# Stick-breaking scores: two rounded products on 128 rows in place of one FP32 product on 64 rows

## The reference

```python
def stick_breaking_attention(q, k, v):          # 8 heads, 512 tokens, 64 wide, for each of 2 layers
    ...
    def block(args):
        qb, qpos = args
        mask = kpos[None, :] < qpos[:, None]
        z = jnp.einsum('bhqd,bhkd->bhqk', qb, k).astype(jnp.float32) * scale     # the scores
        log_beta = jax.nn.log_sigmoid(z)
        log_rem = jnp.where(mask, jax.nn.log_sigmoid(-z), 0.0)
        after = lax.cumsum(log_rem, axis=key_axis, reverse=True) - log_rem
        a = jnp.where(mask, jnp.exp(log_beta + after), 0.0)
        return jnp.einsum('bhqk,bhkd->bhqd', a.astype(v.dtype), v)
```

## Time and profile before

| what | value |
|---|---|
| median of 3 timed runs | 2813.29 us (2812.91 to 2813.4) |
| profiled execution, its span from first to last instruction | 2810.2 us |
| PE busy | 2791.2 us, 99% of the span |
| POOL busy | 2045.0 us, 73% |
| DVE busy | 1325.6 us, 47% |
| ACT busy | 816.3 us, 29% |
| granted PE clock | 0.999 of full speed |
| DMA | 242.59 MB, mean 86 GB/s |

### The profile page before, as it was taken

How to read it: one execution, slowest core, us unless ns; L and a number is a source line. 1 busy time by engine, 2 the same in 40 slices (tenths; PEclk the granted TensorE clock), 3 DMA queues, 4 the chain that set the end, 5 groups by cost and what they waited for, 6 DMA issues and landing times.

```text
span 2810.2 us, 39309 instructions
## 1 busy us (share of the span) xinstructions
PE 2791.2 (99%) x14380; PEld 2253.4 (80%) x14380; DVE 1325.6 (47%) x1878; ACT 816.3 (29%) x1470; POOL 2045.0 (73%) x2353
## 2 busy tenths in 40 slices
PE   9999999999999999999999999999999999999999
PEld 7888888888766888888877788888887777888887
DVE  4945666044675566604764553321074545432201
ACT  3242222024575222202444422110043444211101
POOL 7958988778654899877845587777785456877774
PEclk9999999999999999999999999999999999999999
DMA  4213323323100333322221233323332222333322
GB/s 154 77 54 105 97 96 94 95 96 128 61 2 8 98 97 97 97 96 91 83 68 61 68 98 98 97 96 93 96 97 70 65 66 77 98 97 95 94 96 96
DMA packets 66507, 242.59 MB, mean 86 GB/s; under 512 B 7504, under 2 KB 7632, under 8 KB 66384
## 3 DMA queue, kind: packets, MB, share of 16 engines
q1 hardware_dynamic: 66384, 240.95, 27.1%
HBM read 238.82 MB, written 2.10 MB: 86 GB/s over the span
## 4 chain that ended last, share of the span: by engine, by line
PE 95%; DVE 2%; ACT 2%; issue 1%; DMA 0%; POOL 0%; SPq 0%; DVEq 0%; ACTq 0%
PE bank L546 28%; PE bank L548 28%; PE bank L547 28%; PE bank L1023 1%; PE bank L947 1%; PE bank L1204 1%; PE bank L1120 1%; PE bank L965 1%; PE bank L1163 1%; PE bank L1176 1%; PE bank L1101 1%; ACT n_P L1555 0%; PE bank L602 0%; PE bank L951 0%; PE bank L1091 0%
## 5 line engine op out<-in xcount | busy, mean ns | idle before, releaser
L505 POOL TENSOR_TENSOR w_lo<-w_raw,w_hi 128x256 fp32r<-128x256 f32 x1780 | 1479.1, 862 | 45.6 <-ACT w_hi L1463 10.6
L546 PE MATMUL bank<-XH,w_hi 128*128 128x512 f32 x2416 | 955.4, 395 | 2.2 <-DVE X L2509 1.6
L548 PE MATMUL bank<-XH,w_lo 128*128 128x512 f32 x2416 | 941.2, 390 | 0.0
L547 PE MATMUL bank<-XL,w_hi 128*128 128x512 f32 x2416 | 940.7, 389 | 0.0
L502 POOL CAST w_hi<-w_raw 128x1024 fp32r<-128x1024 f32 x437 | 486.6, 1114 | 618.0 <-DMA w_raw<-weights_dram 617.4
L546 PEld LDWEIGHTS bank<-XH,w_hi 128*128 128x128 f32 x2416 | 453.6, 188 | 103.1 <-issue 9.3
L548 PEld LDWEIGHTS bank<-XH,w_lo 128*128 128x128 f32 x2416 | 453.4, 188 | 96.3
L547 PEld LDWEIGHTS bank<-XL,w_hi 128*128 128x128 f32 x2416 | 453.8, 188 | 93.4 <-issue 2.6
L1822 DVE TENSOR_TENSOR X<-X,bank 128x512 f32<-128x512 f32 x63 | 43.1, 684 | 511.6 <-PE bank L548 511.3
L548 PE MATMUL bank<-hid_h,w_lo 128*128 (+1 forms) x704 | 273.9, 389 | 0.0
L546 PE MATMUL bank<-hid_h,w_hi 128*128 (+1 forms) x704 | 273.9, 389 | 0.0
(11 more groups left out here) (368 smaller groups left out, 3297.3 us busy)
## 6 DMA issues: line engine op xcount, KB each, us to landing
w_raw<-weights_dram SPq DMA_DIRECT2D x445, 512.0 KB, 3.5
x_tok<-x_dram SPq DMA_DIRECT2D x4, 512.0 KB, 5.4
out_dram<-y_tok SPq DMA_DIRECT2D x4, 512.0 KB, 4.1
const_sb<-consts_dram SPq DMA_DIRECT2D x1, 834.0 KB, 11.8
par_sb<-params_dram SPq DMA_DIRECT2D x1, 665.0 KB, 10.3
masks_in<-masks_dram SPq DMA_DIRECT2D x1, 640.0 KB, 12.9
w_raw<-weights_dram SPq DMA_DIRECT2D x2, 256.0 KB, 6.5
y_gain<-gain_out_dram SPq DMA_DIRECT2D x1, 512.0 KB, 4.5
```

The costliest lines, as they stand in the source:

```text
L505: ins = nc.gpsimd.tensor_tensor(w_lo[s][:, rows, :], w_raw[s][:, rows, :], w_hi[s][:, rows, :].bitcast(F32), ALU.subtract)
L546: nc.tensor.matmul(out_ap, w_hi[slot][:, j, :], xh, start=start, stop=False)
L547: nc.tensor.matmul(out_ap, w_hi[slot][:, j, :], xl, start=False, stop=False)
L548: return nc.tensor.matmul(out_ap, w_lo[slot][:, j, :], xh, start=False, stop=stop)
```

## The change

`h_sk` becomes fp32r. For each head, 64 of its rows hold the rounded keys and the other 64 the remainder. The queries of a head lie in two tiles: `h_sqh` holds the rounded query in both halves, `h_sql` the remainder in the half of the rounded keys and zeros in the other. The products `h_sk` x `h_sqh` and `h_sk` x `h_sql` then sum to rounded x rounded, remainder x rounded and rounded x remainder. There are four slots of these pairs (`stack_slot`); two of them lie where `h_dv` was.

- PE (`s_scores`): two rounded products on 128 rows for each key block, in place of one FP32 product on 64.
- ACT: `query_high(h)` makes the rounded queries, two copies of 64x512 for each of eight heads, in place of two for each of four tiles. `key_high(a)` makes the rounded keys from `h_raw`, two copies as before.
- DVE: key tiles 16 to 19 are evicted whole into `h_raw`, in place of two pieces into `h_sk`. `key_low(a)` makes the remainders of two heads, two subtractions. `query_low(h)` is one subtraction a head. `blank_low` writes zeros, two a call, two calls a layer.
- Tiles 18 to 21 may go into `h_raw` only when `key_low` of two tiles earlier is done (`hs["skd"]`).

```diff
-        h_sk = at("h_sk", [P, SB_HEADS, T], F32, o_A + 10240)
+        h_sk = at("h_sk", [P, SB_HEADS, T], F32R, o_A + 10240)
...
-        h_sqs = [at(f"h_sqs{a}", [P, T], F32, o) for a, o in enumerate((o_A + 4096, o_A + 4608, o_A + 5120, o_A + 7168))]
+        sq_places = [o_A + 4096, o_A + 5120, o_A + 6144, o_A + 7168]
+        h_sqh = [at(f"h_sqh{n}", [P, T], F32R, o) for n, o in enumerate(sq_places)]
+        h_sql = [at(f"h_sql{n}", [P, T], F32R, o + T) for n, o in enumerate(sq_places)]
...
+        def stack_slot(h):
+            return h % 2 + 2 * (h // 4)
...
@@ PE, s_scores
-                    pe.wait_ge(hs["sqs"], 4 * ly + h // 2 + 1)
+                    pe.wait_ge(hs["sql"], SB_HEADS * ly + h + 1)
...
-                        mm = nc.tensor.matmul(b[:, lo:lo + SB_W[j]], h_sk[r, h, j * P:(j + 1) * P], queries,
-                                              start=j != 3, stop=False, skip_group_check=True)
+                        keys, slot = h_sk[:, h, j * P:(j + 1) * P], stack_slot(h)
+                        nc.tensor.matmul(b[:, lo:lo + SB_W[j]], keys, h_sqh[slot][:, j * P:T], start=j != 3, stop=False,
+                                         skip_group_check=True)
+                        mm = nc.tensor.matmul(b[:, lo:lo + SB_W[j]], keys, h_sql[slot][:, j * P:T], start=False, stop=False,
+                                              skip_group_check=True)
...
@@ ACT
+                def query_high(h):
+                    act.wait_ge(hs["evac"], U_HYB * ly + 12 + h // 2 + 1)
+                    for to in halves:
+                        ins = nc.scalar.activation(h_sqh[stack_slot(h)][to, :], h_sq[halves[h % 2], h // 2, :], ACT.Copy)
+                    ins.then_inc(hs["sqh"], 1)
...
+                def key_high(a):
...
-                        ins = nc.scalar.activation(h_sk[halves[1 - c], 2 * a + c, :], h_sk[r, 2 * a + c, :], ACT.Copy)
-                    ins.then_inc(hs["skd"], 1)
+                        ins = nc.scalar.activation(h_sk[r, 2 * a + c, :], h_raw[r, a % 2, :], ACT.Copy)
+                    ins.then_inc(hs["skh"], 1)
...
-                        if 12 <= FILL.get(m, 0) < 15:
-                            swapped_query(FILL[m] - 12)
+                        if FILL.get(m, 0) == 12:
+                            query_high(0)
+                            query_high(1)
...
-                swapped_query(3)
+                query_high(2)
...
+                        if h + 3 < SB_HEADS:
+                            query_high(h + 3)
...
@@ DVE, evac
+                        if t in (16, 17):
+                            dve.wait_ge(hs["vT"], 8 * ly + t - 13)
+                        if t in (18, 19, 20, 21):
+                            dve.wait_ge(hs["skd"], 4 * ly + t - 17)
...
+                def query_low(h):
+                    r = halves[h % 2]
+                    dve.wait_ge(hs["sqh"], SB_HEADS * ly + h + 1)
+                    V.tensor_tensor(h_sql[stack_slot(h)][r, :], h_sq[r, h // 2, :], h_sqh[stack_slot(h)][r, :].bitcast(F32),
+                                    ALU.subtract).then_inc(hs["sql"], 1)
+                def blank_low(first):
+                    for n in (first, first + 1):
+                        V.memset(h_sql[n][halves[1 - n % 2], :].bitcast(F32), 0.0)
+                def key_low(a):
+                    dve.wait_ge(hs["skh"], 4 * ly + a + 1)
+                    for c, r in enumerate(halves):
+                        ins = V.tensor_tensor(h_sk[halves[1 - c], 2 * a + c, :], h_raw[r, a % 2, :],
+                                              h_sk[r, 2 * a + c, :].bitcast(F32), ALU.subtract)
+                    ins.then_inc(hs["skd"], 1)
...
@@ DVE, rows of differential attention, after combine(n)
+                    if n == 1:
+                        blank_low(0)
+                    if n == 3:
+                        query_low(0)
+                        query_low(1)
+                    if 16 <= FILL.get(n - 2, 0) < 20:
+                        key_low(FILL[n - 2] - 16)
                     if n in FILL:
                         evac(FILL[n])
...
@@ DVE, heads
                     if h == 0:
                         dve.wait_ge(hs["pv"], 4 * ly + 4)
+                        blank_low(2)
...
+                    if h + 2 < SB_HEADS:
+                        query_low(h + 2)
```

More of the change, by code:

```diff
@@ L419, in build @@
             "evac", "rot", "rope", "vT", "vc", "gate", "lp", "lsum", "le", "lam", "s", "mx", "exp", "w", "t", "tc", "pv",
-            "sqs", "skd", "osq", "on", "ors", "od", "odh", "odl", "z", "ln", "soft", "sphi", "sp", "cum", "a", "spv", "osc", "osh", "osl", "mevac", "mt", "m", "mh",
+            "sqh", "sql", "skh", "skd", "osq", "on", "ors", "od", "odh", "odl", "z", "ln", "soft", "sphi", "sp", "cum", "a", "spv", "osc", "osh", "osl", "mevac", "mt", "m", "mh",
             "ml")}
@@ L1159, in s_scores @@
                         b, lo = region(h, j)
-                        half = j % 2
-                        r = slice(DH * half, DH * (half + 1))
-                        queries = h_sq[r, h // 2, j * P:T] if half == h % 2 else h_sqs[h // 2][r, j * P:T]
-                        mm = nc.tensor.matmul(b[:, lo:lo + SB_W[j]], h_sk[r, h, j * P:(j + 1) * P], queries,
-                                              start=j != 3, stop=False, skip_group_check=True)
+                        keys, slot = h_sk[:, h, j * P:(j + 1) * P], stack_slot(h)
[3 more added lines that the diff above has]
+                                              skip_group_check=True)
                         if j >= 2:
@@ L1674, in hybrid @@
                             v_copy(FILL[m] - 16, 7)
[L1675 to L1676 removed]
+                        if FILL.get(m, 0) == 12:
+                            query_high(0)
+                            query_high(1)
                         if 16 <= FILL.get(m, 0) < 20:
[L1678 removed]
+                            key_high(FILL[m] - 16)
                     if n < 2:
@@ L1723, in hybrid @@
                         softplus_log(1)
+                        query_high(3)
                 def gate(f):
@@ L2339, in evac @@
                     b = bank[t % 5 if t < 12 else fill_bank(t)]
[L2340 to L2346, removed]
+                    if t < 12 or 16 <= t < 24:
                         dst = h_raw[:, t % 2, :]
@@ L2351, in evac @@
                             dve.wait_ge(hs["vT"], 8 * ly + t - 9)
-                        if t >= 20:
+                        if t in (16, 17):
+                            dve.wait_ge(hs["vT"], 8 * ly + t - 13)
+                        if t in (18, 19, 20, 21):
+                            dve.wait_ge(hs["skd"], 4 * ly + t - 17)
+                        if t >= 22:
                             dve.wait_ge(hs["vT"], 8 * ly + t - 17)
@@ L2375, in hybrid @@
                 q0 = units * ly
+                halves = (slice(0, DH), slice(DH, P))
+                def query_low(h):
[12 more added lines that the diff above has]
+                    ins.then_inc(hs["skd"], 1)
                 def combine(m):
```

## The result

The changed kernel took 2816.32 us (median of 21 runs, 2814.74 to 2818.71), the kernel before 2812.89 us beside it (21 runs, 2811.91 to 2814.69 and one of 3989.26). The ratio is 1.0013, with a 95% interval of 1.0007 to 1.0019. The change made the kernel 3.4 us slower. The forecast was 1.7 us faster with a range up to 2815.8 us, and the time lies above it. The profiled execution of the changed kernel took 2817.39 us, 1.1 more than its median.

A forecast was written before the change was run, and what follows sets the result against it. PE, busy 99% of a 2810.2 us span, was taken as the bound; 4.7 us gained on scores less 3.0 lost at tile 20's stop gave 1.7 off 2813.3, so 2811.6 us, with a range of 2808.2 to 2815.8.

The forecast's parts named there:

- A head's scores, 1.26 instead of 1.68: On PE, eight rounded products on 128 rows cost 1.26 us a head instead of 1.68, gaining 0.42.
- heads 3 to 7 keep it: From head 3 on PE does not wait, so 5 x 0.42 = 2.1 us a layer is kept.
- B: Rival: DVE becomes late at the gate eviction behind each fill; 2815.8 us, or 2819 with larger waits; chance 0.13.
- C: Rival: rounded products of all widths go at the 512-column pace, 1.84 us a head; 2818.9 us; chance 0.05.
- Heads 0 to 2 gain 0.25 a layer: Scores of heads 0 to 2: 0.12 + 0.13 = 0.25 us kept a layer instead of 1.26.
- Some 0.3 of head 0's 0.42 goes: At head 0, two blanks (0.9 us) and `query_low(2)` delay DVE; idle of 0.60 us takes up most, some 0.3 is lost.
- Head 1's softplus chain and the fill behind head 2's scores: The fill waits for head 1's softplus, handed over 0.13 us sooner, so two heads' 0.84 becomes 0.13 at most.
- The stop at tile 20, 1.5 us net: PE waits at L602 for `key_low(2)` ahead of the eviction: 1.5 us a layer, 3.0 in all, bounds 0.9 to 2.0.
- the 0.65 for the second subtraction: Of `key_low(2)`'s two DVE subtractions ahead of tile 20's eviction, the first takes 1.1 us, the second 0.65: 1.75.
- The prediction's sentence on the shared port: If DVE and GpSimd operations exclude each other, the first subtraction waits and tile 20's stop is nearer 1.9 than 1.5 us.
- Nothing gives back, and nothing follows: Behind tile 20's stop nothing gives the time back, since PE's stream is its own bound there.
- Blanks and parts in idle time at no cost: Other DVE helpers and ACT's 8 more copies a layer cost nothing; uncovered row 3 up to 0.5 us, layer 0 alone.

The follow-up runs named there:

- e7: The changed kernel with only `blank_low(2)` moved from head 0 to head 1 on DVE: 2813.22 us, ratio 0.9998 to the kernel before.
- c2: The kernel before with two unused 64x512 subtractions on DVE in row 11, ahead of tile 20's eviction: 2816.44 us, ratio 1.0014.
- e1: The changed kernel with value tiles 20 to 23 in two own slots and `key_low(2)`, `key_low(3)` behind their row's eviction: 2809.98 us, ratio 0.9991.
- e2: The changed kernel with `blank_low(2)` moved to head 1 and `query_low(2)` behind head 0's last eviction: 2812.28 us, ratio 1.0000 to the kernel before.
- c1: The kernel before with one unused 64x512 subtraction on DVE in row 11, ahead of tile 20's eviction: 2814.43 us, ratio 1.0008.

## Why the prediction was wrong

Step by step, in its own order.

- **A head's scores, 1.26 instead of 1.68, and heads 3 to 7 keep it.** Right: 1.26 measured, 4.16 us against 4.2, no wait of PE there. Rivals B and C, which attacked this, both fall. B's time (2815.8) lies near the measured one, but by another mechanism.
- **Heads 0 to 2 gain 0.25 a layer.** Here the prediction failed. "Some 0.3 of head 0's 0.42 goes" was the step: it charged the blanks 0.9 us and set the 0.60 us of idle ahead of head 1's scores against them. The idle did give back (0.79 and 0.68), but the lag before it was 2.05 and 1.62. The term left out is what the delay collides with: POOL's cast and subtractions, which add 0.9 us to DVE's chain in layer 0 and 0.45 in layer 1. The three heads together lost 0.86 us in layer 0 and 0.54 in layer 1 in place of a gain of 0.25; beside the forecast that is 1.9 us over both layers. e7 shows that the blanks are the whole cause of this stop.
- **Head 1's softplus chain and the fill behind head 2's scores.** Right in kind: heads 1 and 2 and the fill together gave 0.0 (0.13 forecast, with PE waiting 0.5 instead of 0.8).
- **The stop at tile 20, 1.5 us net.** Right in place and kind, too small in size: 2.0 for the stop less 0.2 for the earlier reduction, 1.8 a layer. The failed number is the 0.65 for the second subtraction. It supposed that POOL ends 0.7 us after DVE begins, as in the earlier trace rows. In the changed kernel POOL began 0.7 us later against DVE's row and took 3.88 us instead of 3.45, so it ended 1.7 us after DVE began, and both subtractions took 1.1. c2 bears this out from the other side: there POOL ended 0.7 us after DVE began, as in the earlier trace rows, and the two took 1.81, near the 1.75 of the prediction. The prediction's sentence on the shared port named 1.9, which came closer than its own 1.5.
- **Nothing gives back, and nothing follows.** This is the other failed step: behind a stop PE was taken to run as before. In the profile it ran at half clock behind two of the four stops, 1.6 us each. That term was in no bound and no rival. c2 shows it without the rest of the change.
- **Blanks and parts in idle time at no cost** (rows 1, 3, 8, 9, 12 and the copies on ACT). Right but for row 3 of layer 0, where `d_values(0)` (L1107) starts 0.2 us later against its partner, under the 0.5 that the prediction allowed; the earlier reduction of row 11 gives it back, so the lag at tile 20's turn has not grown.

Set together for the profile: forecast -1.7, heads 0 to 2 +1.9, tile 20's +0.6, the clock +3.2, start-up +1.3: +5.3 of the +5.4. The timed runs differ by 3.4, so the median run has less of the last two. Without any halved clock the same sum is +0.8, within what a measurement of this kernel tells from no change; the clock made it slower. The timed runs agree. Their mean granted clock averages 0.9979 in the changed kernel (21 runs) and 0.9990 in the kernel before (the 61 runs beside the experiments). By an estimate from these two, 0.0011 of 2815 us is 3.1 us, beside the 2.6 that are missing.

What stays open is when the clock falls. Over the profiles of the changed kernel, e1, e2, e7 and c2 there are twelve stops of 1.6 to 2.1 us. Four were followed by half clock, all of them in layer 0; six stops were in layer 0. Both stops of c1, 0.8 and 1.1 us, were followed by full clock. The Trainium skill (TensorE: Matmul & The Clock Gate, Part 1) says that an idle engine falls back to 1.2 GHz and activity releases it; the trace agrees that the fall comes behind idleness, but not every time. The timed runs show that it differs from one execution of a kernel to the next: the runs of e2 with a mean clock of 0.999, 0.998 and 0.997 (six, four and one) have spans of 2809.8, 2812.1 and 2813.7 us on average, and those of the kernel before beside them 2810.6 at 0.999 and 2813.1 at 0.998. The kernel before has none of these stops and still spreads over 4.1 us, as the changed kernel does over 4.0, so some of the falls come at other places, as at the start-up. Behind which stop the clock fell in a timed run is not on record.

## What to carry to other kernels

Where one engine is busy 99% of the span, a change to its products can be priced closely from its timeline (here a head's scores came out right to 0.01 us, by luck in the single widths, which were off by up to 0.05); the risk is in the helper instructions that the change puts ahead of an eviction on a second engine. Price such a helper with what it pushes later: what the pushed instructions then meet on the third engine, and what the first engine's clock does behind the stop. A helper in a queue belongs behind the last instruction that the bound engine waits for, which here, with two slots more for the value tiles, turned a loss of 3.4 us into a gain of 7.0.

## What the runs showed of the hardware

- A stop of TensorE of 1.6 to 2.1 us can be followed by a stretch at half clock that costs 1.6 us, nearly as much again. That was so behind four of twelve such stops; three of the four were seen with the stop at tile 20 (twice in the kernels of the change, once in c2).
- A DVE copy of 128x128 took 0.22 us alone and 1.05 beside a cast on POOL. The subtractions of 64x512 lie wide apart, and the blanks, which read nothing, all took the same. Three groups of the changed kernel by line (duration in ns: least, median, most; first and last start):

```profile
L2396 DVE MEMSET h_sql<- x8: 485/485/485, 1383.9 to 2234.6; 64x512 f32 x8
...
L2402 DVE TENSOR_TENSOR h_sk<-h_raw,h_sk x16: 685/1102/1180, 1426.3 to 2202.2; 64x512 fp32r<-64x512 f32 x16
...
L2390 DVE TENSOR_TENSOR h_sql<-h_sq,h_sqh x16: 674/1312/1530, 1397.0 to 2319.1; 64x512 fp32r<-64x512 f32 x16
```

The prediction took 0.65 for a subtraction alone; that is about the least of these 32 (0.67), and the middle one took 1.12.

- Of two rounded products of 128 columns behind each other the first cost 0.06 us and the second 0.11.
